# Differential attention's weight units interleaved with its heads, in halves, with the cross attention's value units behind the last head

## What is computed

```python
def diff_attention(h, w_in, w_out, lq1, lk1, lq2, lk2, subln_g, rel_bias, layer_idx):
    q, k, v = jnp.split(h @ w_in, 3, axis=-1)
    q = q.reshape(B, S, 8, 2, 64); k = k.reshape(B, S, 8, 2, 64); v = v.reshape(B, S, 8, 128)
    ...
        logits = jnp.einsum('bqhcd,bkhcd->bhcqk', q_blk, k).astype(jnp.float32) * scale
        logits = logits + bias[None, :, None]
        logits = jnp.where(dist >= 0, logits, -jnp.inf)
        p = jax.nn.softmax(logits, axis=-1)
        attn = p[:, :, 0] - lam * p[:, :, 1]
        return jnp.einsum('bhqk,bkhd->bqhd', attn.astype(v.dtype), v)
    ...
    o = rmsnorm(o, subln_g) * (1.0 - lam_init)
    return o.reshape(B, S, D_MODEL).astype(h.dtype) @ w_out

def mem_cross_attention(h, mem_n, w_q, w_kv, w_o):
    q = (h @ w_q).reshape(B, S, CA_HEADS, CA_HEAD_DIM)
    k, v = jnp.split(mem_n @ w_kv, 2, axis=-1)
    ...
# per layer:
    x = x + mix
    x = x + mem_cross_attention(rmsnorm(x, norm_cross[i]), mem_n, ca_w_q[i], ca_w_kv[i], ca_w_o[i])
    x = x + swiglu(rmsnorm(x, norm_ffn[i]), ffn_w_gu[i], ffn_w_down[i])
```

## Time and profile before

| | us |
|---|---|
| median of three runs | 3071.54 (3068.43 to 3073.09) |
| profiled execution, its span | 3072.0 |
| PE busy | 2858.2 (93%) |
| DVE busy | 1955.8 (64%) |
| ACT busy | 1369.3 (45%) |

### The profile page before, as it was taken

One profiled execution on the slowest core, in us unless ns is written; L12 is line 12 of the kernel. 1 busy time (PEld: TensorE's weight loads), 2 busy tenths in 40 slices (PEclk: granted clock), 3 DMA queues, 4 the chain that ended last, 5 costly groups with the idle time before them and its releaser, 6 DMA issues.

```text
span 3072.0 us, 50729 instructions
## 1 busy us (share of the span) xinstructions
PE 2858.2 (93%) x21031; PEld 2695.5 (88%) x21031; DVE 1955.8 (64%) x2718; ACT 1369.3 (45%) x1640; POOL 0.7 (0%) x5
## 2 busy tenths in 40 slices
PE   5999889999998899979999979999989999979998
PEld 5899879999996799969899978989989899959897
DVE  5887767868759555555466665566655666555665
ACT  3335434343353444444444514444544545444443
POOL 0000000000000000000000000000000000000000
PEclk7899979999998899979999999999999999979999
DMA  8987417968953155624255623345654456514453
GB/s 236 317 279 244 137 42 251 291 225 294 292 186 97 54 194 175 222 82 140 92 194 176 210 80 116 119 165 187 196 165 137 148 181 211 186 52 128 159 171 109
DMA packets 458799, 533.02 MB, mean 174 GB/s; under 512 B 9879, under 2 KB 435081, under 8 KB 458633
## 3 DMA queue, kind: packets, MB, share of 16 engines
q1 hardware_dynamic: 457340, 530.11, 52.9%
q10 hardware_dynamic: 1293, 0.65, 0.1%
HBM read 528.10 MB, written 2.62 MB: 173 GB/s over the span
## 4 chain that ended last, share of the span: by engine, by line
PE 83%; DVE 10%; ACT 3%; issue 2%; DMA 2%; SPq 1%; ACTq 0%; DVEq 0%
PE ps L1902 14%; PE ps L1735 11%; PE ps L1887 11%; PE ps L2190 8%; PE ps L1717 6%; PE ps L1719 6%; PE ps L1718 6%; PE ps L1888 5%; PE ps L1765 2%; PE ps L1764 2%; PE ps L1763 2%; PE ps L1971 2%; PE ps L1942 2%; DMA work<-in_ada_w 1%; DVE work L1451 1%
## 5 line engine op out<-in xcount | busy, mean ns | idle before, releaser
L1074 DVE TENSOR_TENSOR wlo<-raw,whi 128x2048 fp32r<-128x2048 f32 (+1 forms) x514 | 976.6, 1919 | 474.3 <-ACT whi L709 474.0
L709 ACT ACTIVATE whi<-raw 128x2048 fp32r<-128x2048 f32 (+1 forms) x514 | 824.8, 1611 | 409.5 <-PE ps L1719 112.2
L1887 PE MATMUL ps<-parts_f,whi 128*128 128x512 f32 x1408 | 503.3, 401 | 10.9 <-issue 10.9
L1717 PE MATMUL ps<-hhi,whi 128*128 128x256 f32 x1360 | 390.3, 287 | 16.1 <-issue 13.4
L1888 PE MATMUL ps<-parts_f,wlo 128*128 128x256 f32 x1408 | 396.8, 282 | 0.0
L1718 PE MATMUL ps<-hlo,whi 128*128 128x256 f32 x1360 | 387.6, 285 | 0.0
L1719 PE MATMUL ps<-hhi,wlo 128*128 128x256 f32 x1360 | 387.5, 285 | 0.0
L1902 PE MATMUL ps<-ghi,whi 128*128 128x256 f32 x1280 | 362.3, 283 | 3.0 <-DVE wlo L1074 3.0
L1902 PE MATMUL ps<-glo,whi 128*128 128x256 f32 x1280 | 362.2, 283 | 0.0
L1902 PE MATMUL ps<-ghi,wlo 128*128 128x256 f32 x1280 | 362.1, 283 | 0.0
L1887 PEld LDWEIGHTS ps<-parts_f,whi 128*128 128x128 f32 x1408 | 266.2, 189 | 76.3 <-issue 12.6
(11 more groups left out here) (259 smaller groups left out, 4851.2 us busy)
## 6 DMA issues: line engine op xcount, KB each, us to landing
raw<-in_ffn_w_in SPq DMA_DIRECT2D x88, 1024.0 KB, 8.8
raw<-in_ffn_w_gu SPq DMA_DIRECT2D x88, 1024.0 KB, 5.1
work<-in_ada_w SPq DMA_DIRECT2D x72, 1024.0 KB, 8.8
raw<-in_ffn_w_out SPq DMA_DIRECT2D x88, 512.0 KB, 5.7
raw<-in_ffn_w_down SPq DMA_DIRECT2D x88, 512.0 KB, 5.6
raw<-in_ca_w_kv SPq DMA_DIRECT2D x32, 1024.0 KB, 5.7
raw<-in_mix_w_in SPq DMA_DIRECT2D x24, 1024.0 KB, 6.2
raw<-in_da_w_in SPq DMA_DIRECT2D x24, 1024.0 KB, 5.5
```

Of the source, the lines that this page charges most:

```text
L709: f(whi[:, s, 0:size], raw[:, s, 0:size], ACT.Copy).then_inc(hi_done[s], 1)
L1074: tt(wlo[:, s, 0:size], raw[:, s, 0:size], whi[:, s, 0:size].bitcast(F32), ALU.subtract).then_inc(lo_done[s], 1)
L1717: mm(dst, wh, xh, start=first, stop=False)
L1887: mm(ps[:, banks[m], :], th[:, k, c], parts_f[:, :, k, :], start=k == 0, stop=False)
```

## The change

- The 12 units of differential attention come in the order dq, dk, dv of the first pair of heads, then of the second pair, and so on (`DIFF_ORDER`). The four value units `xv` of the cross attention, in layers 0 and 3 alone, follow them in the stream and belong to the stage diff. These 16 units write bank 0 or 1 by turns, whatever their slot; `Unit.b` is the bank.
- The first five units are multiplied before the first head (`LEAD`). Then TensorE goes round: scores of head j; the first half (24 matmuls, 128 of the 256 columns or rows) of unit 5+j; turn of head j-1; in odd rounds from 3 on the column sums of a pair; the second half; values of head j-1. Units 13, 14 and 15 follow head 7.
- ScalarE and VectorE copy unit 4+j and split a unit ahead inside round j. Scores have banks 4 and 5 alone; scores of head j wait until head j-1 is masked.
- The mixer's result goes into `fhi`, `flo` in the place of `hhi`, `hlo`, which the units still read. In the work area `xv` and `xq` change places.
- The wait of SyncE for the bias table stands at stage diff, ahead of the same units as before.

```diff
+        DIFF_ORDER = (("dq", 0, 0), ("dk", 1, 0), ("dv", 2, 0), ("dq", 0, 1), ("dk", 1, 1), ("dv", 2, 1), ("dq", 0, 2),
+                      ("dk", 1, 2), ("dv", 2, 2), ("dq", 0, 3), ("dk", 1, 3), ("dv", 2, 3))
+        LEAD = 5
...
+                st.own = [plan.column(w, at * D, name, n, turn % 2, token_major=at == 2)
+                          for turn, (name, at, n) in enumerate(DIFF_ORDER)]
+                last_use[0] = st.own[-1]
+                st.mem = [plan.column(wkv, D, "xv", n, n % 2, token_major=True) for n in range(4)]
...
-            vunits = project("cross", plan.columns(wkv, D, 4, "xv", token_major=True), src="mem")
+            if i % 3:
+                vunits = project("cross", plan.columns(wkv, D, 4, "xv", token_major=True), src="mem")
...
(ScalarE)
+                for j in range(8):
+                    evict(us[LEAD - 1 + j])
+                    ahead(us[LEAD + j].pos)
+                    if j >= 4 and j % 2 == 0:
+                        high((j - 4) // 2)
+                    if j >= 3 and j % 2:
+                        squares((j - 3) // 2)
+                    exps(j)
+                    if j:
+                        turned_out(j - 1)
+                    if j >= 3 and j % 2:
+                        root(st.gn + (j - 3) // 2, 2, 2 * HD, d_rs)
...
(VectorE)
+                for j in range(8):
+                    maxima(j)
+                    if j >= 4 and j % 2 == 0:
+                        low((j - 4) // 2)
+                    evict(us[LEAD - 1 + j])
+                    ahead(us[LEAD + j].pos)
+                    probabilities(j)
+                    if j >= 3 and j % 2:
+                        normed((j - 3) // 2)
...
(TensorE)
+                for u, src in us[:LEAD]:
+                    unit(u, src, st.h)
+                for b in (2, 3):
+                    pe.wait_ge(read[b], st.reads[b])
+                for j in range(8):
+                    scores(j)
+                    half(*us[LEAD + j], 0)
+                    if j:
+                        turn_head(j - 1)
+                    if j >= 3 and j % 2:
+                        pair_sum((j - 3) // 2)
+                    half(*us[LEAD + j], 1)
+                    if j:
+                        values(j - 1)
+                half(*us[LEAD + 8], 0)
+                turn_head(7)
+                half(*us[LEAD + 8], 1)
+                values(7)
+                half(*us[LEAD + 9], 0)
+                pair_sum(3)
+                half(*us[LEAD + 9], 1)
+                unit(*us[LEAD + 10], st.h)
```

More of the change, by code:

```diff
@@ L167, in __init__, with unit @@
         self.stages = []
-    def unit(self, src, size, what, cols=256, token_major=False, bank=True):
+    def unit(self, src, size, what, cols=256, token_major=False, bank=True, b=None):
         s = self.slot
-        u = Unit(len(self.stream), s, self.uses[s], self.reads[s], what, cols, token_major, bank)
+        b = s if b is None else b
+        u = Unit(len(self.stream), s, self.uses[s], self.reads[b], what, cols, token_major, bank, b)
         self.stream.append((s, self.uses[s], src, size))
         self.uses[s] += 1
-        self.reads[s] += bank
+        self.reads[b] += bank
         self.slot = (s + 1) % SLOTS
@@ L379, in out_project @@
             stages.append(Stage(kind="out", mixer=stages[-1], units=units, mod=mod, i=take("out")))
-            return [(read[u.slot], u.read + 1) for u in units]
+            return [(read[u.b], u.read + 1) for u in units]
         def ffn(w_in, w_out, mod=None, ada=None):
@@ L662, in _ @@
                     stream(st.pos + 2 + 4 * (STEPS - 1) + 2)
-                elif st.kind in ("project", "mix1", "hgrn_out", "out"):
-                    if st.kind == "project" and st.name == "diff":
-                        d = next(t for t in stages if t.kind == "diff" and t.units is st.units)
-                        sp.wait_ge(q["ffn_lo"], STEPS * (3 + d.layer) + 1)
+                elif st.kind in ("project", "mix1", "hgrn_out", "out", "diff"):
+                    if st.kind == "diff":
+                        sp.wait_ge(q["ffn_lo"], STEPS * (3 + st.layer) + 1)
                         sp.wait_ge(q["bias_out"], 16)
@@ L1606, in tree8 @@
+                ahead(us[LEAD + 8].pos)
+                evict(us[LEAD + 8])
+                ahead(us[LEAD + 9].pos)
+                normed(3)
+                evict(us[LEAD + 9])
+                low(3)
+                ahead(us[LEAD + 10].pos)
+                evict(us[LEAD + 10])
             def tree8(st):
@@ L1743, in unit @@
                 if u.read > 0:
-                    pe.wait_ge(read[u.slot], u.read)
+                    pe.wait_ge(read[u.b], u.read)
                 for e in extra:
@@ new lines, in half @@
+            def half(u, src, m):
+                if m == 0:
+                    weights(u)
+                    if u.read > 0:
+                        pe.wait_ge(read[u.b], u.read)
+                    if src == "mem":
+                        pe.wait_ge(q["norm_lo"], 8)
+                xh, xl = h_parts(src)
+                th, tl = tiles(u.slot, u.cols)
+                c = slice(P * m, P * m + P)
+                dst = ps[:, u.b, 256 * m:256 * m + 256]
+                for k in range(KT):
+                    first, last = k == 0, k == KT - 1
+                    if u.token_major:
+                        mm(dst, xh[:, k, c], th[:, k, :], start=first, stop=False)
+                        mm(dst, xh[:, k, c], tl[:, k, :], start=False, stop=False)
+                        o = mm(dst, xl[:, k, c], th[:, k, :], start=False, stop=last)
+                    else:
+                        o = product(dst, (th[:, k, c], tl[:, k, c]), xh[:, k, :], xl[:, k, :], first, last)
+                if m == 1:
+                    o.then_inc(used[u.slot], 1)
```

242 lines of the change are left out of this document (129 added, 113 removed).

## The result

The changed kernel takes 2998.18 us (median of 4 runs, 2995.48 to 3000.28), against 3071.78 us (4 runs, 3068.43 to 3073.09) of the kernel before. The ratio is 0.9766, with a 95% interval of 0.9754 to 0.9779: 2.3% faster. In a second measurement beside other kernels it was 2999.34 us and 0.9771 (0.9757 to 0.9784). The forecast of 2987 us was 11 us too low, and the time lies in the range.

A forecast was written before the change was run, and what follows sets the result against it. Two differential stages, latency chains across three engines, cost 120.16 us; filled, 17.04 + 0.84 + 0.1 = 18.0 each, 36.0 for both. Gain 84.2 from 3072.0 gives 2987.8, the median 0.5 lower: 2987 us, range 2980 to 3010.

The forecast's parts named there:

- The chain of latencies: Differential stages of layers 0 and 3: latencies across three engines cost 60.41 and 59.75 us above the units, together 120.16 us.
- Head products: TensorE's scores, turns, values and column sums stay, paid at full clock: 17.04 us per stage.
- Seams: 28 head pieces set mostly inside units cost 0.03 us each, by one inserted piece in a memory unit: 0.84 us per stage.
- The estimate that I gave by the Trainium skill: Isolated matmuls take about 0.17 us above their columns: 4.8 us per stage for 28 pieces, total some 8 us higher.
- Waits: TensorE in the stage: only head 6's scores wait, for ScalarE's copy of the last pair's key, 0.1 us a stage.
- The cover of the four value units: Moving the xv units from between the norm's statistics and its first reader exposes no wait: cost 0.
- VectorE keeps up: Over a stage's eight rounds VectorE has 53.6 us of work against TensorE's 61.3, with 3 us to spare at the turn.
- Rival B: VectorE sets the round in the differential stages, 9.1 us against TensorE's 7.7: 22 us more, 3010 us; chance 0.09.
- ScalarE's copies have the time of half a unit: Rounds of the differential stage: ScalarE is lighter than VectorE, 2.5 us a head, and a split adds 1.90.
- Clock: With TensorE filled in the differential stages, the granted clock is 1.00 throughout, and the first output unit loses its slow start.
- rival C: The granted clock stays at 0.50 from unit 5 to 15 of the stages: slower than before, up to 3150 us; chance 0.04.
- Rival A: Every change between fp32r and float32 products drains TensorE, 0.36 us each: 18.5 us more in all, 3006 us; chance 0.09.

The follow-up runs named there:

- e8_rows128: e1 with two more float32 matmuls of 256 columns over 128 rows ahead of each head's turn in the differential stages: 3008.28 us.
- e1: The changed kernel with ScalarE's copy of the first key unit put right behind the norm's exponential, ahead of the copies of the normed rows: 2991.46 us.
- e2: The changed kernel with the two banks of all units of the differential stage exchanged in layer 3 alone: 2998.97 us.
- e4: e1 with cross attention's four value units back behind the second key unit, only the mixer's own 12 units going between heads: 3007.53 us.
- e5: e1 with VectorE forming a quarter (512 of 2048 columns) of its weight split's low part twice in each round: 2990.63 us.
- e6: e1 with VectorE forming the whole low part (2048 columns) of its weight split twice in each round: 2998.21 us.
- e3: e1 with the halves undone, a whole unit standing between scores and the turn of the head before: 3003.18 us.
- e7: e1 with two more float32 matmuls of 256 columns over 64 rows ahead of each head's turn in the differential stages: 3010.52 us.

## Why the prediction was right, and where it fell short

**The chain of latencies: right.** The stage lost its idle time and its low clock, and nearly the whole gain comes from it: 40.8 us in layer 0, where 60.41 - 18.0 = 42.4 had been forecast. From the start of unit 0 to the last addition TensorE is busy for all but 0.1 us in layer 0's stage.

**Head products: right at the turn and the sums, and the scores' row was misread.** Turn 0.32, sums 0.86 a pair and the values' own 0.65 came as reckoned. The 0.73 of the earlier trace rows is from scores to scores: there is no change of rows between them.

**Seams: the term that was mis-sized.** I took 28 x 0.03 = 0.84 us from an inserted piece that goes over 128 rows and has no such change in it. The runs show 20 seams that cost nothing (turns, values against units, sums) and 8 scores at 0.31 us, 2.5 us a stage. This makes 17.04 + 2.5 + 0.16 = 19.7 us above the units, where 19.65 were measured on TensorE. Against the forecast 18.0 it is 1.65 us a stage, 3.3 us in all. The estimate that I gave by the Trainium skill (TensorE: Matmul & The Clock Gate, Single matmul latency) was 4.8 us, too much, and put on the wrong pieces: e8_rows128's inserted pieces cost 0.87 us, their columns alone. The page that does bear on it is another one of the Trainium skill, TensorEngine Tiling (Array Packing), Key Properties: it says that changing the tiling mode drains the engine. The traces fit it, with 0.34 us for there and back, lost at the changes and not between them; that a drain is the reason no run here shows. I hadn't weighed it.

**Waits: right in the rounds, wrong at the head of layer 3's stage.** The scores of head 6 waited for the last key's copy, once a stage, and 0.1 us had been allowed. From the second values matmul (1341.82) they start after 0.47 us, in place of 0.31:

```profile
1341.82 0.38 PE L2043 MATMUL ps<-work 128*128 128x128 f32 x2
1342.29 0.50 PE L2172 MATMUL ps<-work 64*128 64x128 f32 x4
```

What I left out is the bank of unit 0 in layer 3. It is the case that I had named as the sign of being wrong, a wait at a seam on one of the copies of more than 0.1 us. Of the stage's start I had looked only at the norm and its readers, not at who had last used the bank that unit 0 now takes, and on which engine that copy is queued. This step cost 3.77 us of idle time and 1.39 of low clock, 5.2 us (e1, e2). The two profiled executions are 74.0 us apart where 84.2 had been forecast. Of these 10.2 us, the wait and the seams make 5.2 + 3.3 = 8.5. The rest lies where nothing was meant to change: 1.1 ahead of layer 0's stage (1265.85 in place of 1264.77) and 1.2 between the two stages, less 0.6 gained behind layer 3's; its causes were not looked for. The other 0.8 of the 11 us are the medians' distance from the profiled executions.

**The cover of the four value units: right.** Cost 0 forecast, 0.07 us measured (e4).

**VectorE keeps up: right,** with 3.97 us to spare at the last turn, where 3 had been reckoned: 11 us more of work cost nothing, 37 us cost 7 (e5, e6). Rival B is out.

**ScalarE's copies have the time of half a unit: right in the rounds.** Without the halves, 5.7 us a stage are lost (e3).

**Clock: right in the rounds.** It is 1.00 in all of them, so rival C didn't come; it was half only behind the wait in layer 3. The 16 units go round two banks without harm in layer 0. The rule of the Trainium skill on cycling through banks (TensorE: Matmul & The Clock Gate, A second HAM failure mode: psum-queue depth-cycling) didn't show. It tells of small idle gaps between groups of products, and TensorE was busy for 40.00 of 40 us here. In e3, whose stage in layer 0 has five gaps of 0.63 us and one of 1.31, the clock stayed at 1.00 too.

**Rival A** was right that seams cost more, and wrong in how: 0.36 us a piece for all 28 would be 10 us a stage, and 2.5 were found. Only the scores' two changes together come to the 0.3 us that I had named as its mark. The 0.36 itself was misread. The turn at 1341.79 stands where the clock falls (granted 0.68 from 1341.70 to 1342.50, 0.50 in the us behind), and the scores behind it are a change of rows; I had held it against transposes at full clock. How much each made isn't shown.

**The range.** Its low end was added up wrong: 2987 - 3 - 1.7 is 2982, not 2981. Nothing hangs on it.

## What to carry to other kernels

A stage that is a chain of latencies across engines is filled by independent products, and gives back its idle time and its low clock together; count what is left as products at full clock, plus the changes of array rows between them. When an order of units is changed, look at each unit's bank: who used it last, which engine copies it out, and what is queued on that engine ahead of the copy. Here the copy that frees a bank belonged ahead of the eight copies of the normed rows, as ScalarE was idle there anyway. Judge changes of a few us by the length of the stage in the trace, where they repeated within 0.1 us here, while the whole time varied by 8.

## What was not expected of the hardware

- A change from float32 or fp32r products over 128 rows to products over 64 rows of the array and back costs TensorE 0.34 us in sum (e7 against e8; 0.31 in a round), all of it at the changes. A change between fp32r and float32 over 128 rows costs nothing that shows: two matmuls set into a unit cost 0.87 us for 0.86 us of columns.
- An idle time of 3.77 us in a stretch that was full before and after brought the granted clock to half for some 3 us behind it, which cost 1.39 us more; 6.04 us cost 1.81 more. Waits of up to 1.31 us in a full stage (e3) left it at 1.00.
